# Mamba's decay rows: a product with 64 rows of the array against one with 128, the rest filled with zeros

## The chip, the cores and the metric

The kernel runs on one core of one Trainium2 chip. The metric is the device time of one execution in microseconds (us), as the median of several runs.

## The reference

The kernel computes ten layers in one launch, on 256 tokens of width 1024 in float32: feed-forward layers, one Mamba-2 mixer and three attention mixers, each behind an RMS norm with shift and scale, and each added to the residual with a gate. The change touches the Mamba mixer alone. What matters of it (SSM_CHUNK is 256, so the 256 tokens are one chunk; there are 8 groups of 4 heads):

```python
def step(state, inp):
    x_k, dt_k, b_k, c_k = inp
    acum = jnp.cumsum(dt_k * a, axis=1)
    seg = acum[:, :, None] - acum[:, None, :]
    decay = jnp.exp(jnp.where(causal, seg, -jnp.inf))
    cb = jnp.einsum('btgn,bsgn->btsg', c_k, b_k)
    w = cb[..., None] * decay * dt_k[:, None]
    y_intra = jnp.einsum('btsgr,bsgrp->btgrp', w, x_k)
    ...
```

For each of the 32 heads there is thus a matrix of 256 x 256 decays, exp(acum[t] - acum[s]) for t >= s.

## The kernel before

Float32 products are made out of float32r ones: each operand is split into a high part and a rest, and three products (high x high, high x rest, rest x high) are added in one bank of PSUM. Weights come from DRAM as blocks of 128x2048 through six buffers (`raw`). ScalarE copies a block to its high part (`w_hi`, L495), VectorE subtracts that to get the rest (`w_lo`, L913), both two blocks ahead of TensorE. A third of a block's products are on L1573, L1574 and L1575 each (for the first slice of the inner dimension L1630, L1631 and L1632), with 128 rows, 128 columns of weights and 256 columns that stream.

Each engine has its own program, written out by hand, and works through it in order; engines wait for one another on counters, one per kind of step. `k.wait(name, ...)` waits for such a counter and `k.inc(name, instruction)` raises it.

**The Mamba stage** is the second of ten. It runs a first part and then seven groups of the same form (`body`), each with four blocks of weights. TensorE's program of a group is: the product for x of this group into bank 4; `more_rows`, the decay rows of heads 2 and 3 of the group ahead; the product for B and C into bank 5; `y_out`, the output of the group ahead (L1857, L1858); the product for z into bank 7; `parts`, transposes and C.B (L1832 to L1837); `gemm_out`, the output product of the group before; `first_rows`, the decay rows of heads 0 and 1 of this group. Behind the last group come `more_rows` and `y_out` once more.

**Decay rows** are made by `rows`. The cumulative sums of all 32 heads lie in `acT`, heads on partitions: the high parts on partitions 0 to 31, the rests on 32 to 63. For each group VectorE multiplies them by a column of ones and zeros that keeps the group's four heads (`group_rows`, L1296) and writes `acg`, 64 x 384. The 384 columns are tokens 0 to 255 and once more 128 to 255, for the two halves of the matrix with only what is not above the diagonal. For head h TensorE multiplies `acg` by the selector `sel[:, h * 128:(h + 1) * 128]`, which has a one where a partition's head is h modulo 4: that spreads the head's row (high part plus rest) over all 128 partitions of the bank (L1822). A second product with bf16 operands adds a large negative number above the diagonal: `ident_b` and `below_b`, both in the tile `conb`, 256 columns (L1825). ScalarE then takes the exponential of the bank with a bias for each partition (L650), and VectorE multiplies it by C.B (L1264). `first_rows` and `more_rows` call `rows` twice each, so these products come in pairs, 16 pairs in all.

The selector and the mask are made once, in the first stage, by `mixer_constants`: on ScalarE (L472 to L477, `sel` from the constant `mod4`) and on VectorE (L903, L905). The constant `mod4` is laid out with 128 partitions, of which 64 to 127 hold zeros:

```python
k = np.arange(64)[:, None] % 32
put("mod4", k % 4 == np.arange(4)[None, :])
```

TensorE's wait for the counters `const` and `late` comes at the end of the first stage.

Of the kernel before, what the change touches and what calls it, by code (L numbers as in the profile page):

```python
# [20 lines left out]
F32 = mybir.dt.float32  # L21
F32R = mybir.dt.float32r
# [5 lines left out]
P = 128  # L28
# [222 lines left out]
def build(nc, weights, mods, params, consts, xin, out, stages=None):  # L251
# [3 lines left out]
    with ExitStack() as ctx:  # L255
        def sb(name, shape, dt=F32):
            return ctx.enter_context(nc.sbuf_tensor(name, shape, dt))
# [29 lines left out]
        small = sb("small", [P, 12])  # L287
        cact = sb("cact", [P, NJOB * 8])
        rstd = sb("rstd", [P, T])
        sel = sb("sel", [64, 512], F32R)  # L290

        acg = sb("acg", [64, 384], F32R)[:, :]
        a_hi = sb("a_hi", [P, 2, T], F32R)
        a_lo = sb("a_lo", [P, 2, T], F32R)
        z_hi, z_lo = h_hi[:, 1:3, :], h_lo_rest[:, 0:2, :]
# [31 lines left out]
        def par_(name, at=0, n=None):  # L327
            o, w = PARAMS[name]
            return par[:, o + at:o + at + (w if n is None else n)]

        def con_(name, rows=P):
            o, w = CONSTS[name]
            return con[0:rows, o:o + w]
# [120 lines left out]
        def _(eng):  # L454
# [13 lines left out]
            def mixer_constants():  # L468

                eng.wait_ge(s_con, 16)  # L470
                eng.wait_ge(s_par, 16)
                eng.activation(ident_b, con_("ident"), ACT.Copy)  # L472
                eng.activation(above_b, con_("triL"), ACT.Copy, scale=-NEG)
                m4 = con_("mod4", 64)
                eng.activation(sel[:, :].rearrange("p (h c) -> p h c", h=4), m4.unsqueeze(2).to_broadcast([64, 4, P]),
                               ACT.Copy)
                eng.activation(ws_hi[:, :], par_("wsmall"), ACT.Copy).then_inc(sems["const"], 1)  # L477

# [56 lines left out]
            def ffn(st):  # L535
# [23 lines left out]
                for n in range(1, NFB):  # L559
                    gate(n, 3, -1)  # L560
                    up(n, 3, 0)
                    down(n, 3, 1)
                    if st == 0 and n == GATE_AT:
                        mixer_constants()
                    if st == 0 and n == GATE_AT + 1:
                        gate_weights(1)
# [328 lines left out]
        def _(eng):  # L895
# [4 lines left out]

            def mixer_constants():
                eng.wait_ge(s_con, 16)
                eng.tensor_scalar(below_b, con_("tri"), 1.0, -NEG, ALU.subtract, ALU.mult).then_inc(sems["late"], 1)  # L903
                eng.wait_ge(sems["const"], 1)
                eng.tensor_tensor(ws_lo[:, :], par_("wsmall"), ws_hi[:, :], ALU.subtract).then_inc(sems["late"], 1)  # L905
# [197 lines left out]
            def ffn(st):  # L1103
# [26 lines left out]
                for n in range(1, NFB):  # L1130
                    gate(n, 3, -1)
                    gather(st, n, "gate")
                    up(n, 3, 0)
                    gather(st, n, "up")
                    if st == 0 and n == GATE_AT + 1:
                        mixer_constants()
                    down(n, 3, 1)
                    gather(st, n, "down")
# [416 lines left out]
        def _(eng):  # L1555
# [232 lines left out]
            def mamba(st):  # L1788
# [29 lines left out]
                def rows(i, off, h, free):  # L1818

                    free()  # L1820
                    b = bank[6 + h % 2]
                    eng.matmul(b[:, 0:384], sel[:, h * P:(h + 1) * P], acg, start=True, stop=False,  # L1822
                               skip_group_check=True)
                    diag = b[:, :].rearrange("p (a b c) -> p a b c", a=2, b=2)[:, :, 0, :]
                    k.inc("br", eng.matmul(diag, ident_b, below_b.unsqueeze(1).to_broadcast([P, 2, P]),  # L1825
                                           start=False, stop=True, skip_group_check=True))
# [12 lines left out]
                def first_rows(i):  # L1839
                    if i == 0:  # L1840
                        k.wait("acv", st, b=2)
                    k.wait("acg", st, i, 1, 0)
                    rows(i, 0, 0, lambda: k.wait("y1", st, i, 1, -1))
                    rows(i, 0, 1, lambda: k.wait("sil", st, i, 3, 2))

                def more_rows(i):
                    rows(i, -1, 2, lambda: k.wait("dec", st, i, 4, -4))
                    rows(i, -1, 3, lambda: k.wait("dec", st, i, 4, -3))
# [387 lines left out]
```

## Time and profile before

| | |
|---|---|
| median of 3 runs | 1782.38 us (1781.78 to 1782.6) |
| span of the profiled execution, first to last instruction | 1789.0 us |
| its mean granted clock of TensorE | 0.999 |
| TensorE busy | 1749.9 us (98%) |
| VectorE busy | 1452.8 us (81%) |
| ScalarE busy | 956.5 us (53%) |
| moved from DRAM | 423.74 MB, 239 GB/s over the span |

For the profiled execution no time is given beside its span, which is 6.6 us longer than the median of the runs. Durations below are of that execution. A busy engine is one with an instruction in hand: the records of products overlap, since the next one starts to stream before the one ahead has left the array, so the distance from start to start tells more than a product's own length.

### The profile page before, as it was taken

The page shows a single profiled execution, that of the slowest core. Times are in us where ns is not written, and L with a number is a line of the kernel's source. Part 1 is how long each engine was busy: PE and PEld are TensorE (multiplying, and loading weights), DVE is VectorE, ACT ScalarE, POOL GpSimd, SP SyncE. Part 2 cuts the span into 40 slices and gives each one's busy share as a digit, 9 for nine tenths or more (in the row PEclk, how much of TensorE's full clock was granted, in tenths as well). Part 3 has the DMA queues.
Part 4 walks back from the last instruction along what each step waited for, and adds up shares of the span by engine and source line. Part 5 has one row for each costly group of instructions (what it writes and reads, how often), then busy time and mean ns, then how long its engine had stood idle before and what let it go on. Part 6 is the DMA issues. An engine that isn't in the chain of part 4 may idle for free.

```text
span 1789.0 us, 34260 instructions
## 1 busy us (share of the span) xinstructions
PE 1749.9 (98%) x14686; PEld 1700.5 (95%) x14686; DVE 1452.8 (81%) x1749; ACT 956.5 (53%) x1254; POOL 0.2 (0%) x4
## 2 busy tenths in 40 slices
PE   5999999999999999999999999999999999999999
PEld 4999999998999999999999999999999998989999
DVE  7799898888898889898557989765899887567766
ACT  4443466665533354445766444565655556775553
POOL 0000000000000000000000000000000000000000
PEclk9999999999999999999999999999999999999999
DMA  9998834344597949895444989343288545415551
GB/s 396 414 419 307 322 141 154 134 173 154 219 410 312 373 167 386 326 393 193 170 152 186 388 329 378 134 163 139 110 304 292 206 147 177 151 73 214 187 197 37
DMA packets 68149, 426.23 MB, mean 238 GB/s; under 512 B 7488, under 2 KB 10832, under 8 KB 31824
## 3 DMA queue, kind: packets, MB, share of 16 engines
q1 hardware_dynamic: 63936, 416.22, 60.5%
q10 hardware_dynamic: 4112, 8.62, 1.4%
q8 instruction: 68, 1.11, 0.2%
q14 instruction: 33, 0.27, 0.0%
HBM read 423.74 MB, written 3.17 MB: 239 GB/s over the span
## 4 chain that ended last, share of the span: by engine, by line
PE 90%; DVE 4%; ACT 3%; DMA 2%; issue 0%; DVEq 0%; SPq 0%; ACTq 0%
PE bank L1573 24%; PE bank L1574 24%; PE bank L1575 24%; PE bank L1630 2%; PE bank L1632 2%; PE bank L1631 2%; DMA raw<-weights 1%; PE bank L1686 1%; PE bank L1989 1%; DMA mix<-mods 1%; PE bank L1586 1%; PE bank L1600 1%; PE bank L1589 1%; PE bank L1822 1%; ACT w_hi L495 1%; DVE work L1034 1%
## 5 line engine op out<-in xcount | busy, mean ns | idle before, releaser
L1573 PE MATMUL bank<-h_hi,w_hi 128*128 128x256 f32 x2504 | 696.0, 278 | 0.0
L1574 PE MATMUL bank<-h_lo_rest,w_hi 128*128 128x256 f32 x2504 | 694.9, 278 | 0.0
L1575 PE MATMUL bank<-h_hi,w_lo 128*128 128x256 f32 x2504 | 694.8, 277 | 0.0
L913 DVE TENSOR_TENSOR w_lo<-raw,w_hi 128x2048 fp32r<-128x2048 f32 x267 | 609.5, 2284 | 90.4 <-ACT w_hi L495 89.3
L495 ACT ACTIVATE w_hi<-raw 128x2048 fp32r<-128x2048 f32 x276 | 527.9, 1913 | 160.0 <-PE bank L1575 145.7
L1573 PEld LDWEIGHTS bank<-h_hi,w_hi 128*128 128x128 f32 x2504 | 472.8, 189 | 0.0
L1574 PEld LDWEIGHTS bank<-h_lo_rest,w_hi 128*128 128x128 f32 x2504 | 470.2, 188 | 0.0
L1575 PEld LDWEIGHTS bank<-h_hi,w_lo 128*128 128x128 f32 x2504 | 470.1, 188 | 0.0
L1573 PE MATMUL bank<-a_hi,w_hi 128*128 128x256 f32 x1280 | 358.5, 280 | 1.2 <-DVE a_lo L1291 0.8
L1575 PE MATMUL bank<-a_hi,w_lo 128*128 128x256 f32 x1280 | 355.3, 278 | 0.0
L1574 PE MATMUL bank<-a_lo,w_hi 128*128 128x256 f32 x1280 | 355.3, 278 | 0.0
L1573 PEld LDWEIGHTS bank<-a_hi,w_hi 128*128 128x128 f32 x1280 | 241.9, 189 | 3.4 <-issue 1.4
L1574 PEld LDWEIGHTS bank<-a_lo,w_hi 128*128 128x128 f32 x1280 | 240.4, 188 | 0.1
L1575 PEld LDWEIGHTS bank<-a_hi,w_lo 128*128 128x128 f32 x1280 | 240.4, 188 | 0.0
L968 DVE SCALAR_TENSOR_TENSOR macc<-modws,cact,macc 128x1536 f32<-128x1536 f32 x126 | 225.8, 1811 | 1.8 <-DMA modws<-mods 1.8
L1154 DVE SCALAR_TENSOR_TENSOR mix<-bank,par,mix 128x254 f32<-128x254 f32 (+1 forms) x176 | 76.7, 477 | 41.6 <-ACT mix L581 40.0
L1630 PE MATMUL bank<-h_lo_first,w_hi 128*128 128x256 f32 x344 | 100.1, 291 | 1.6 <-DVE work L1376 1.4
L554 ACT ACTIVATE a_hi<-mix 128x512 fp32r<-128x512 f32 x40 | 25.3, 633 | 140.6 <-PE bank L1575 125.3
L1632 PE MATMUL bank<-h_hi,w_lo 128*128 128x256 f32 x344 | 97.9, 285 | 0.0
L1631 PE MATMUL bank<-h_hi,w_hi 128*128 128x256 f32 x344 | 96.6, 281 | 0.0
L581 ACT ACTIVATE mix<-bank,par 128x256 f32<-128x256 f32 x88 | 44.9, 561 | 92.2 <-PE bank L1575 92.2
L540 ACT ACTIVATE mix<-bank 128x512 f32<-128x512 f32 x44 | 26.4, 599 | 116.8 <-PE bank L1575 116.8
(303 smaller groups left out, 1989.4 us busy)
## 6 DMA issues: line engine op xcount, KB each, us to landing
raw<-weights SPq DMA_DIRECT2D x276, 1024.0 KB, 5.4
modws<-mods SPq DMA_DIRECT2D x144, 768.0 KB, 6.6
mix<-mods SPq DMA_DIRECT2D x5, 1024.0 KB, 8.8
mix<-mods ACTq DMA_DIRECT2D x8, 512.0 KB, 13.3
biases<-scratch ACTq DMA_DIRECT2D x1, 2048.0 KB, 13.1
mix<-biases ACTq DMA_DIRECT2D x4, 512.0 KB, 4.0
modws<-mods SPq DMA_DIRECT2D x1, 1024.0 KB, 11.7
x<-xin SPq DMA_DIRECT2D x1, 1024.0 KB, 10.9
```

The costliest lines, as they stand in the source:

```text
L495: eng.activation(w_hi[g % NW][:, :], raw[g % NRAW][:, :], ACT.Copy).then_inc(sems["whi"], 1)
L540: k.inc("silu", eng.activation(sg, bank[4][:, :].rearrange("p (a t) -> p a t", a=2), ACT.Silu))
L581: ins = eng.activation(dst[:, m, :], b[:, m * T:(m + 1) * T], ACT.Identity, scale=cw(i, t, 2), bias=cw(i, t, 3))
L913: eng.tensor_tensor(w_lo[g % NW][:, :], raw[g % NRAW][:, :], w_hi[g % NW][:, :], ALU.subtract).then_inc(sems["wlo"], 1)
L968: ins = eng.scalar_tensor_tensor(out=m, in0=modw[q % 4], scalar=c, in1=m, op0=ALU.mult, op1=ALU.add)
L1154: ins = eng.scalar_tensor_tensor(out=dst[:, m, lag:T], in0=b[:, m * T:(m + 1) * T - lag], scalar=cw(i, 22 * up + m, tap), in1=dst[:, m, la ...
L1573: eng.matmul(dst, ah, bh, start=start, stop=False, skip_group_check=skip)
L1574: eng.matmul(dst, ah, bl, start=False, stop=False, skip_group_check=skip)
L1575: return eng.matmul(dst, al, bh, start=False, stop=stop, skip_group_check=skip)
L1630: eng.matmul(d, hi[:, kk, part], h_lo(kk), start=True, stop=False)
L1631: eng.matmul(d, hi[:, kk, part], h_hi[:, kk, :], start=False, stop=False)
L1632: eng.matmul(d, lo[:, kk, part], h_hi[:, kk, :], start=False, stop=False)
```

## The change

Both operands of the selector product get 128 partitions. `sel` and `acg` are declared with 128; `acg` stays as the name of the lower 64, into which VectorE writes as before. Partitions 64 to 127 of `sel` are written with the zeros of `mod4` by the same copy on ScalarE, and those of `acg` are cleared once by a new instruction of VectorE. The product takes all 128 partitions of both. The upper half adds zero times zero. No instruction changes its place on any engine, and no wait is added: VectorE has one instruction more, a memset of 64x384 in `mixer_constants`, ahead of the mask constant.

```diff
@@ build @@
-        sel = sb("sel", [64, 512], F32R)
-
-        acg = sb("acg", [64, 384], F32R)[:, :]
+        sel = sb("sel", [P, 512], F32R)
+
+        acg_all = sb("acg", [P, 384], F32R)[:, :]
+        acg = acg_all[0:64, :]
@@ ScalarE, mixer_constants @@
-                m4 = con_("mod4", 64)
-                eng.activation(sel[:, :].rearrange("p (h c) -> p h c", h=4), m4.unsqueeze(2).to_broadcast([64, 4, P]),
+                m4 = con_("mod4")
+                eng.activation(sel[:, :].rearrange("p (h c) -> p h c", h=4), m4.unsqueeze(2).to_broadcast([P, 4, P]),
                                ACT.Copy)
@@ VectorE, mixer_constants @@
                 eng.wait_ge(s_con, 16)
+                eng.memset(acg_all[64:P, :].bitcast(F32), 0.0)
                 eng.tensor_scalar(below_b, con_("tri"), 1.0, -NEG, ALU.subtract, ALU.mult).then_inc(sems["late"], 1)
@@ TensorE, rows @@
-                    eng.matmul(b[:, 0:384], sel[:, h * P:(h + 1) * P], acg, start=True, stop=False,
+                    eng.matmul(b[:, 0:384], sel[:, h * P:(h + 1) * P], acg_all, start=True, stop=False,
                                skip_group_check=True)
```

## Rows read from the trace of the kernel before

**Rows 1.** The page: span, and busy time, share of the span, instructions by engine.

```profile
span 1789.0 us, 34260 instructions
PE 1749.9 (98%) x14686; PEld 1700.5 (95%) x14686; DVE 1452.8 (81%) x1749; ACT 956.5 (53%) x1254; POOL 0.2 (0%) x4
```

**Rows 2.** The page: the chain that ended last, by engine.

```profile
PE 90%; DVE 4%; ACT 3%; DMA 2%; issue 0%; DVEq 0%; SPq 0%; ACTq 0%
```

**Rows 3.** Busy time by stretches: where the memset comes, and one group of Mamba.

```profile
core 0: us, PE busy (x) PEld busy (x) DVE busy (x) ACT busy (x) POOL busy (x), PEclk, DMA share, GB/s
...
64.00:80.00 16.00, 15.64 (x135) 15.45 (x135) 15.22 (x14) 8.58 (x11) 0.00 (x0) 1.00 1.00 413
...
304.00:331.00 27.00, 27.00 (x224) 25.32 (x224) 23.40 (x34) 17.57 (x23) 0.00 (x0) 1.00 0.41 157
```

**Rows 4.** Timeline of TensorE's products around one pair: start us, us, what.

```profile
303.52 0.28 PE L1574 MATMUL bank<-a_lo,w_hi 128*128 128x256 f32 x1
303.63 0.28 PE L1575 MATMUL bank<-a_hi,w_lo 128*128 128x256 f32 x1
303.84 0.44 PE L1822 MATMUL bank<-acg,sel 64*128 64x384 f32 x1
304.21 0.28 PE L1825 MATMUL bank<-conb 128*128 128x256 bf16 x1
304.43 0.44 PE L1822 MATMUL bank<-acg,sel 64*128 64x384 f32 x1
304.80 0.28 PE L1825 MATMUL bank<-conb 128*128 128x256 bf16 x1
...
305.04 0.28 PE L1631 MATMUL bank<-h_hi,w_hi 128*128 128x256 f32 x1
```

**Rows 5.** Timeline of the weight loads (PEld) of the same stretch.

```profile
303.52 0.19 PEld L1575 LDWEIGHTS bank<-a_hi,w_lo 128*128 128x128 f32 x1
303.84 0.18 PEld L1822 LDWEIGHTS bank<-acg,sel 64*128 64x128 f32 x1
304.21 0.10 PEld L1825 LDWEIGHTS bank<-conb 128*128 128x128 bf16 x1 [0.19 <-issue]
...
304.80 0.20 PEld L1630 LDWEIGHTS bank<-h_lo_first,w_hi 128*128 128x128 f32 x1
```

**Rows 6.** Timelines of other stages: bf16 of 384 columns, and plain f32.

```profile
1501.57 0.33 PE L1946 MATMUL bank<-conb 128*128 128x384 bf16 x1
1501.73 0.28 PE L1908 MATMUL bank<-con,mix 128*128 128x1 f32 x2
...
1171.26 0.59 PE L1961 MATMUL bank<-mix,con 128*128 128x256 f32 x2
1171.69 0.27 PE L1962 MATMUL bank<-mix,con 128*128 128x128 f32 x1
```

**Rows 7.** The selector product: ns min/median/max, first and last start.

```profile
L1822 PE MATMUL bank<-acg,sel x32: 407/439/442, 249.2 to 442.2; 64*128 64x384 f32 x32
```

**Rows 8.** Timeline of TensorE at the first pair.

```profile
249.24 0.41 PE L1822 MATMUL bank<-acg,sel 64*128 64x384 f32 x1 [1.15 <-DVE acg L1296]
...
250.40 0.28 PE L1631 MATMUL bank<-h_hi,w_hi 128*128 128x256 f32 x1
```

**Rows 9.** Timeline at the last two pairs: exponentials, and the third selector product.

```profile
440.77 2.84 ACT L650 ACTIVATE work<-bank,mix 128x256 f32<-128x256 f32 x8 [3.44 <-PE bank L1825]
...
441.55 0.44 PE L1822 MATMUL bank<-acg,sel 64*128 64x384 f32 x1 [0.24 <-ACT work L650]
```

**Rows 10.** Timelines of VectorE and TensorE in the group behind the first.

```profile
269.07 0.69 DVE L1291 TENSOR_TENSOR a_lo<-work,a_hi 128x512 fp32r<-128x512 f32 x1
...
270.95 0.36 PE L1573 MATMUL bank<-a_hi,w_hi 128*128 128x256 f32 x1
```

**Rows 11.** VectorE: the multiply of 64x384, and a wait in the first stage.

```profile
L1296 DVE TENSOR_SCALAR acg<-mix,con x8: 400/403/413, 248.7 to 429.9; 64x384 fp32r<-64x384 f32 x8
...
94.92 1.82 DVE L968 SCALAR_TENSOR_TENSOR macc<-modws,cact,macc 128x1536 f32<-128x1536 f32 x1 [0.70 <-DMA modws<-mods]
```

## The prediction

> **What bounds the kernel now.** The shares of the page come first: TensorE is busy for 98% of the span, VectorE for 81% [rows 1]. The chain that ended last runs over TensorE for 90% of its length [rows 2]. So nearly every microsecond that TensorE spends is one of the kernel, whether it multiplies or only stands between two products, as long as the others keep up. The table by stretches then shows the place of the change: in one group of the Mamba stage (27 us, seven such groups follow the first) TensorE is busy throughout at a granted clock of 1.00, while VectorE works 23.4 us of them and ScalarE 17.6 [rows 3]. Busy is not the same as streaming, though. For that one reads the timeline, start by start.
>
> The timeline of one pair of decay rows [rows 4] holds the argument. In the big products 256 columns follow each other every 0.11 us (303.52 to 303.63). Then the steps are: last big product to the first selector product 0.21; selector product to mask product (L1825) 0.37; mask to second selector product 0.22; selector to mask 0.37; mask to the second big product behind it 0.24, in which lie two products of 256 columns, so no pause. Both steps *into* a selector product (64 rows) are 0.10 to 0.11 longer than what 256 columns take, and both steps *out* of it are long as well. The loads say why [rows 5]: the load of a full product starts while the one ahead streams (303.52 for the product at 303.63; the load at 304.80 starts together with the mask product ahead of it), and these loads take 0.19 us at a distance of 0.11. The two loads next to a selector product do not: the selector's load starts 0.21 after the product ahead, and the mask's load stands idle for 0.19 us behind the selector, in which no other engine is named. What distinguishes the three is the number of rows, 64 against 128.
>
> **What the change does, part by part.**
>
> *The product with 128 rows.* Its columns stay 384. The nearest row with 384 columns and full rows is a bf16 product of another stage: 0.16 us from start to start (1501.57 to 1501.73) [rows 6]. Float32r streams as bf16 does, since 256 columns take 0.11 in both. I take 0.16. The other end: plain f32 products with full rows take 0.43 for two of 256 columns (1171.26 to 1171.69) [rows 6], twice as long a column, so 0.32 for 384.
>
> *The pauses.* If they belong to the change between 64 and 128 rows, a pair becomes 0.11 + 0.16 + 0.11 + 0.16 + 0.24 = 0.78 us, where rows 4 have 1.41 (303.63 to 305.04): 0.63 us saved, namely 0.10 + 0.21 + 0.11 + 0.21. The page on tiling of the Trainium skill (TensorEngine Tiling (Array Packing), Key Properties) says that changing the tiling mode drains TensorE; by that rule the trace agrees. The same skill also speaks against the change: TensorE: Matmul & The Clock Gate, in its table on why this matters, has a product of few rows take the same time as one of 128, by which filling up rows would bring nothing and the time would stay 1782.4. That is the first rival below.
>
> *How many.* There are 32 selector products [rows 7], 16 pairs; 13 stand between big products as in rows 4 and read alike to 0.01 us. 13 x 0.63 = 8.2. The first pair waits 1.15 us for VectorE's decay rows and then takes 1.16 (249.24 to 250.40) [rows 8]; after the wait it would take 0.67, 0.5 saved. The last two pairs stand back to back, and behind them ScalarE's exponentials run without a break for 2.84 us [rows 9]; the third selector product and what follows wait for those. There only what lies ahead of the first exponential counts: one step in and one out, 0.3. Sum: 8.2 + 0.5 + 0.3 = 9.0 us.
>
> *What is late next.* The groups become 1.26 us shorter, 26 instead of 27.25, against 23.4 us of VectorE's work [rows 3]: it has idle time left. It is tightest in the group behind the first, where VectorE runs without a pause: its rest of the gated output (L1291) ends at 269.76, and TensorE begins the product that reads it at 270.95 [rows 10], 1.2 us later. By then TensorE is ahead by 0.5 + 0.6 = 1.1. That eats the slack almost wholly; with the signal between the engines I put 0.1 us of waiting. In later groups TensorE gains at most 1.26 per group while VectorE's own inputs come earlier too, since they hang on TensorE; I cost these at nothing, and if that cover is gone it is rival two.
>
> *The added clearing on VectorE.* One memset of 64x384 ahead of the mask constant, before the Mamba stage. No row shows one; above it is bounded by the multiply of the same shape, 0.40 us [rows 11], below by nothing much, say 0.1. I take 0.3, nearer to the same shape. It comes at about 79 us, where VectorE is busy 15.2 of 16 us and the DMA queues are full [rows 3]. Behind it stand the splitting of weights and the accumulation that frees modulation buffers; a later free buffer is a later transfer, and lost DMA time there is not regained at once. But VectorE waits 0.70 us for such a transfer at 94.92 [rows 11], so most is absorbed. Between 0 and 0.4, I take 0.1. The selector's copy on ScalarE has as many elements in each row as before and more rows: nothing, and if it did cost, ScalarE is the engine with the most idle time.
>
> So 9.0 - 0.1 - 0.1 = 8.8 us. The profiled execution spans 1789.0 us, 6.6 above the median of the runs, 1782.4; the pauses are differences within it, and I subtract them from the median: **1773.6**. About 0.2%, 3.6 us, is what a measurement of this kernel can tell from no change, so faster means below 1778.8.
>
> **The rivals.**
>
> *No gain: the pause isn't of rows.* The long steps could belong to the order float32r, bf16, float32r with different shapes, or to the bank the pair writes twice. For it: every selector product stands beside a mask product. Against: the mask product is followed by a full float32r product without pause (304.80 to 305.04), and the step into the selector from a float32r product (0.21) is the same as from a bf16 one (0.22). Time: 1782.4 plus at most 0.4 for the clearing, 1782.6. Chance 0.08.
>
> *The gain is made on TensorE and partly eaten.* If VectorE, now at 23.4 of 26 us, makes TensorE wait about 0.5 us in each of seven groups (the gap at rows 10 fully used, again and again), 3.5 go: 8.8 - 3.5 = 5.3, 1777.1. For: VectorE takes its work in order, with weights to split in the middle. Against: no wait of TensorE between 276 and 440. Chance 0.08.
>
> *Half the pauses stay.* Suppose the selector's load cannot be pulled ahead even with full rows. Then the steps in remain: 13 x 0.21, 0.1 in the first pair and 0.1 in the last, about 2.9; the gain is 5.9 and the time 1776.5. The reverse, that only the steps in go, gives 1779.5. TensorE: Matmul & The Clock Gate of the Trainium skill (Part 3, What overlaps and what doesn't) has weight loads overlap running products only where their row groups differ; by that rule the full load would stay exposed, but rows 5 show full loads overlapping full products. Chance 0.08 for both, half on each side of 1778.8.
>
> *Slower: the full product streams at the rate of plain f32.* The place is L1822, the price 32 x (0.32 - 0.16) = 5.1 us of TensorE time. It decides the sign if the pauses don't go: 1782.4 + 5.1 = 1787.5; if they go, it leaves 1778.7. For it only the longer record of the selector product [rows 7], against it the float32r products with full rows at 0.11 for 256 columns [rows 4]. Chance 0.04 for the first.
>
> **How the numbers follow.** The forecast has what is left, 0.72. Its own bounds: 16 x 0.63 = 10.1 with nothing eaten gives 1772.3; with the spread of the runs (0.4) and a step a little shorter than I took, 1771.5. The range reaches up over the two partial cases to 1779.0 and leaves out no gain (0.08), slower (0.04) and a bit of the partial ones. Faster: 0.72 + 0.08 + 0.04 = 0.84. Within 0.2%: 0.08 + 0.04 = 0.12. Slower: 0.04.
>
> **What would show it.** In the profile of the changed kernel the mask's load should have no idle time before it, the steps around a pair should read 0.11, 0.16, 0.11, 0.16, and the distance between the same places of two groups 26.0 us instead of 27.25. The first rival shows unchanged steps of 0.37; the second shows short steps and new waits of TensorE for VectorE in the Mamba stage; the third short steps on one side alone; the fourth a step of 0.32 behind the selector. I am wrong if a pair takes over 1.0 us, or if TensorE's waits in the stage grow by more than a microsecond.

## The result, and the profile after

The median of 21 executions is 1773.94 us, against 1783.16 us for 21 of the kernel before. The ratio of changed to before is 0.9953, with a 95% interval from 0.9939 to 0.9967: some 8.4 us, or 0.47%, faster, and clear of the 0.2% that a measurement can tell. The forecast was 1773.6 us. Both medians are raised by executions in which a stage ran at a slower pace (below), 10 of 21 before and 7 of 21 with the change. The others have medians of 1782.01 and 1773.55 us, 8.5 apart.

The page of the changed kernel, its span, the busy times and the chain that ended last (lines from 287 on have moved by one or two: L1822 is L1824, L1825 is L1827):

```profile
span 1782.0 us, 34261 instructions
PE 1742.4 (98%) x14686; PEld 1699.3 (95%) x14686; DVE 1452.5 (82%) x1750; ACT 956.5 (54%) x1254; POOL 0.2 (0%) x4
...
PE 93%; DVE 3%; ACT 3%; DMA 1%; issue 0%; DVEq 0%; SPq 0%; ACTq 0%
```

But for the one memset the instructions are what they were, and so is the bound [rows 1, 2]; TensorE is busy for 7.5 us less. The timeline of TensorE around one pair of decay rows, to be laid beside [rows 4]:

```profile
303.79 0.28 PE L1577 MATMUL bank<-h_hi,w_lo 128*128 128x256 f32 x1
303.90 0.34 PE L1824 MATMUL bank<-acg,sel 128*128 128x384 f32 x1
304.09 0.28 PE L1827 MATMUL bank<-conb 128*128 128x256 bf16 x1
304.12 0.42 PE L1824 MATMUL bank<-acg,sel 128*128 128x384 f32 x1
304.39 0.28 PE L1827 MATMUL bank<-conb 128*128 128x256 bf16 x1
...
304.63 0.28 PE L1633 MATMUL bank<-h_hi,w_hi 128*128 128x256 f32 x1
```

And its weight loads, to be laid beside [rows 5]:

```profile
303.80 0.19 PEld L1824 LDWEIGHTS bank<-acg,sel 128*128 128x128 f32 x1
304.08 0.10 PEld L1827 LDWEIGHTS bank<-conb 128*128 128x128 bf16 x1
304.09 0.20 PEld L1824 LDWEIGHTS bank<-acg,sel 128*128 128x128 f32 x1
```

The selector's load now starts together with the big product ahead of it, and the mask's load has lost its idle time, in all 32 cases. (Single steps inside the pair read oddly: the second selector is recorded 0.03 us behind the mask, and 0.27 lie between it and the next mask. From mask to mask it is 0.30.) The pair takes 304.63 - 303.79 = 0.84 us instead of 1.41. One group behind another comes after 26.09 us (297.70 to 323.79 for the same place) instead of 27.25.

**Which part of two profiles can be compared.** The spans of the two profiled executions differ by 7.0 us, but they can't be subtracted. Every feed-forward stage runs, from its start to its end, at one of two paces, and which one it is changes from execution to execution, in both kernels alike. The number of big products that start in 100 us shows it: first before, then changed, a stretch in the first and one in the sixth stage (us, TensorE busy and in brackets the products, clock, DMA share, GB/s).

```profile
80.00:180.00 100.00, 100.00 (x852) 1.00 0.94 368
970.00:1070.00 100.00, 100.00 (x880) 1.00 0.89 350
```

```profile
80.00:180.00 100.00, 100.00 (x879) 1.00 0.96 377
970.00:1070.00 100.00, 100.00 (x852) 1.00 0.90 349
```

From start to start that is 117.8 against 114.0 ns a product on average (a window also counts the products under way at its start), 3.7 us up to the first selector product where the first stage was hit (249.24 against 245.50), some 5 us in a later stage; the slower pace had hit the first stage of the one profile and the sixth of the other (and the third of both). So the change is read within Mamba alone: from the first selector product to the first product of the last output it is 443.03 - 249.24 = 193.79 us before and 430.93 - 245.50 = 185.43 us after. That is 8.36 us less, about the measured gain of 8.4.

Not all of it is the change. Mamba has the two paces too, there for each stretch of some 45 big products between two interruptions. The kernels differ in this only in the first three stretches: from the first pair to the second the kernel before takes 255.81 - 250.40 = 5.41 us and the changed one 251.62 - 246.36 = 5.26, and in the next two the differences cancel. So 0.15 us is pace. Another 0.09 is gone again a few products later: read to the second pair of heads of the last output, at 443.76 and 431.75, the difference is 8.27. The change is worth **8.1 us** within the stage.

### The profile page after: what moved, and what is told of

The parts are those of the page before. It is cut to its first block, busy times and chain, and to the rows that moved or that the text cites. A ratio compares the mean times of both kernels' runs of the same rounds, so it can differ in the third digit from the quotient of the medians.

```text
span 1782.0 us, 34261 instructions
## 1 busy us (share of the span) xinstructions
PE 1742.4 (98%) x14686; PEld 1699.3 (95%) x14686; DVE 1452.5 (82%) x1750; ACT 956.5 (54%) x1254; POOL 0.2 (0%) x4
## 4 chain that ended last, share of the span: by engine, by line
PE 93%; DVE 3%; ACT 3%; DMA 1%; issue 0%; DVEq 0%; SPq 0%; ACTq 0%
PE bank L1575 25%; PE bank L1576 24%; PE bank L1577 24%; PE bank L1632 2%; PE bank L1634 2%; PE bank L1633 2%; PE bank L1588 1%; PE bank L1688 1%; PE bank L1602 1%; PE bank L1991 1%; DMA mix<-mods 1%; PE bank L1591 1%; ACT w_hi L496 1%; PE bank L1859 1%; ACT work L719 0%; PE bank L1972 0%
## 5 line engine op out<-in xcount | busy, mean ns | idle before, releaser
L541 ACT ACTIVATE mix<-bank 128x512 f32<-128x512 f32 x44 | 26.4, 600 | 117.8 <-PE bank L1577 117.7
```

Source lines behind the costliest of these rows:

```text
L541: k.inc("silu", eng.activation(sg, bank[4][:, :].rearrange("p (a t) -> p a t", a=2), ACT.Silu))
```

## The experiments

A pair, below, is the time from the start of the last big product ahead of it to the start of the second one behind it: 1.41 us before, 0.84 us with the change. The pairs of one kernel agree to about 0.01 us. Single times of executions are given but carry no verdict, since an execution may hold stages at the slower pace (up to two in the profiled ones).

### All four products of a pair on 64 rows (e1_mask64)

From the kernel before. The mask product takes 64 rows as well, with operands of its own; both diagonal blocks are then blanked instead of masked.

```diff
-                    k.inc("br", eng.matmul(diag, ident_b, below_b.unsqueeze(1).to_broadcast([P, 2, P]),
+                    k.inc("br", eng.matmul(diag, fold_b[:, :], neg_b[:, :].unsqueeze(1).to_broadcast([64, 2, P]),
```

> Kernel before, with the mask product also on 64 rows, so that all four products of a pair have 64 rows. It leaves out the right mask: both diagonal blocks are blanked instead. Read from the start of the last big product ahead of a pair to the second behind it (before: 1.41 us, changed kernel: 0.84). Theory A, the pause belongs to the change between 64 and 128 rows: only one step in and one out are left, 0.21 + 0.17 + 0.11 + 0.17 and about 0.45 at the way out, 1.1 us in all, and the mask's load stands idle no more behind the selector inside the pair. Theory B, the pause belongs to the selector product or to the alternation of float32r and bf16: the steps of 0.37 stay, 1.4 us.

Measured (1779.22 us, once). The timeline of TensorE around a pair; L1825 is the selector, L1828 the mask:

```profile
278.15 0.28 PE L1578 MATMUL bank<-h_hi,w_lo 128*128 128x256 f32 x1
278.35 0.44 PE L1825 MATMUL bank<-acg,sel 64*128 64x384 f32 x1
278.64 0.28 PE L1828 MATMUL bank<-neg_b,fold_b 64*128 64x256 bf16 x1
278.94 0.28 PE L1828 MATMUL bank<-neg_b,fold_b 64*128 64x256 bf16 x1
279.15 0.39 PE L1633 MATMUL bank<-h_lo_first,w_hi 128*128 128x256 f32 x1
279.37 0.28 PE L1634 MATMUL bank<-h_hi,w_hi 128*128 128x256 f32 x1
```

The pair takes 1.22 us. Inside it float32r and bf16 still take turns, but the first selector is followed by its mask after 0.29 instead of 0.37 and the second mask comes 0.30 behind the first, exactly as in the changed kernel (304.09 to 304.39). The pauses are now at the two ends: 0.20 on the way in, and on the way out the full product's load waits until 279.15. So neither the selector product as such nor the change of types has the price; the change of size has it. Theory A's 1.1 us was short by 0.12, all of it at the first selector: from there to its mask it is 0.29 us, not the forecast 0.17, while the way out takes 0.43 (forecast 0.45). On the way in the selector starts 0.09 late, and its own load of 0.18 us then costs another 0.11. So the pause holds the load of the next product, and its price goes with that load. A change ahead of a float32r load (0.18 to 0.19 us) costs 0.20 here on the way in and 0.19 on the way out. A change ahead of the mask's bf16 load (0.10 us) costs 0.08, the 0.37 of the kernel before less these 0.29. Twice 0.20 and twice 0.08 make 0.56, the excess of 0.57 of the pair before.

### Half as many changes of size (e2_adjacent)

From the kernel before, same results: the two selectors of a pair stand next to each other.

```diff
-                    eng.matmul(b[:, 0:384], sel[:, h * P:(h + 1) * P], acg, start=True, stop=False,
-                               skip_group_check=True)
+                    last = h % 2
+                    for step in (("spread", "mask") if last else ("mask", "spread")):
...
```

> Kernel before, same products and results, in the order mask, selector, selector, mask instead of selector, mask, selector, mask. Theory A: two changes of size a pair instead of four: 0.11 + 0.22 + 0.16 + 0.37 + 0.24 = 1.10 us instead of 1.41, a gain of 0.3 a pair, about 4.5 us in the stage. Theory B, a fixed price for each 64-row product: 1.41 as before. If the price sits in the alternation of types, also 1.10, which e1 then tells apart (there the types still alternate).

Measured (1779.86 us, once). The timeline of TensorE; L1826 stands for both selectors, with one mask ahead of them and one behind:

```profile
306.65 0.28 PE L1575 MATMUL bank<-h_hi,w_lo 128*128 128x256 f32 x1
...
306.98 0.61 PE L1826 MATMUL bank<-acg,sel 64*128 64x384 f32 x2
...
307.77 0.28 PE L1631 MATMUL bank<-h_hi,w_hi 128*128 128x256 f32 x1
```

1.12 us, forecast 1.10. The same four products on the same rows, with two changes of size instead of four: half the excess over 0.84 is gone (0.28 is left of 0.57). A change costs 0.14 us here, on average; by e1 it is 0.20 into the selectors and 0.08 out of them.

### 96 rows (e3_rows96)

From the changed kernel; `sel[0:96, ...]` and `acg_all[0:96, :]` in the product.

> Changed kernel, but the selector product takes 96 rows instead of 128 (results the same). If up to 64 rows count as one size and more as full, the pair takes 0.84 us as in the changed kernel. If every row count short of 128 has its own size, the pauses are back: 1.41 us.

Measured (1777.54 us, once). The timeline of TensorE:

```profile
277.27 0.28 PE L1577 MATMUL bank<-h_hi,w_lo 128*128 128x256 f32 x1
277.39 0.34 PE L1824 MATMUL bank<-acg,sel 96*128 96x384 f32 x1
...
278.12 0.28 PE L1633 MATMUL bank<-h_hi,w_hi 128*128 128x256 f32 x1
```

0.85 us: 96 rows count as full ones. What mattered was not to fill up to the last row but to leave the size of 64 behind. Between 65 and 95 nothing was tried.

### Only heads 0 and 1 (e4_first_only)

From the changed kernel; `r = slice(0, P if h < 2 else 64)` picks the rows of both operands.

> Changed kernel with full rows for heads 0 and 1 alone (the pairs of first_rows); the pairs of more_rows go back to 64 rows. One part alone, both kinds in one trace: first_rows 0.84 us, more_rows 1.41, a group 26.67 us (27.25 before, 26.09 changed), the first selector product to the last output 4.1 us less than before instead of 8.4. If the gain came from anything set up once (the clearing, the wider copy), both kinds would read alike.

Measured (1782.11 us, once). In one trace, first_rows and then the next more_rows:

```profile
272.01 0.28 PE L1577 MATMUL bank<-a_hi,w_lo 128*128 128x256 f32 x1
272.12 0.34 PE L1825 MATMUL bank<-acg,sel 128*128 128x384 f32 x1
...
272.85 0.28 PE L1633 MATMUL bank<-h_hi,w_hi 128*128 128x256 f32 x1
```

```profile
278.10 0.28 PE L1577 MATMUL bank<-h_hi,w_lo 128*128 128x256 f32 x1
278.30 0.44 PE L1825 MATMUL bank<-acg,sel 64*128 64x384 f32 x1
...
279.50 0.28 PE L1633 MATMUL bank<-h_hi,w_hi 128*128 128x256 f32 x1
```

0.84 and 1.40 us, side by side. Five groups take 411.43 - 278.10 = 133.33 us, 26.67 each, as expected; first selector to last output is 434.89 - 245.33 = 189.56 us, 4.2 less than before. Nothing that is set up once has a part in the gain. (The time of this one execution shows no gain: its eighth stage ran at the slower pace, which costs what the four microseconds gave.)

### The preparation alone (e5_clear_only)

From the changed kernel; the product goes back to `sel[0:64, ...]` and `acg`, the clearing and the wider copy stay.

> Changed kernel with the wider selector copy and the clearing of the upper half kept, but the selector product back on 64 rows (results the same): the cost of the preparation alone. Theory A: pairs of 1.41 us as before, groups of 27.25, the memset takes 0.38 us of VectorE and nothing of the end: equal to the kernel before within its spread. A rival, that the memset's delay of weight splitting or of the transfers behind it costs up to 0.4 us or more, would show as new waits of TensorE in the first stage.

Measured: ratio to before 1.0007, interval 0.9994 to 1.002. Pairs of 1.41 us (306.31 to 307.72), and the mask's load again idle for 6.0 us in 32 cases. The memset takes 0.38 us of VectorE; TensorE waits for nothing in the first stage that it did not wait for in other kernels without it. From the first selector product to the last output it takes 193.80 us, 193.79 before. In the trace the preparation costs nothing. The times are a weaker witness: the interval reaches up to 0.2%, 3.6 us, since 8 of the 12 executions lie near 1787 us, as 9 of the 23 of the kernel before do; the other four lie at 1781.1 to 1783.1. Whether that share is chance was not looked into.

### Masks behind both selectors (e6_masks_last)

From the changed kernel: selector, selector, mask, mask, through a function `pair` in place of the two calls of `rows`.

> Changed kernel with the order selector, selector, mask, mask in a pair instead of selector, mask, selector, mask (same results). A pair takes 0.84 us where its streaming gives 0.78. If the remaining 0.06 comes from the bf16 weights behind a float32r product (twice a pair, loads of 0.10 that start only when the selector's stream ends), one such step is left and a pair takes about 0.81. If it comes from the longer stream of the selector alone, 0.84 stays.

Measured (1775.71 us, once). The timeline of TensorE:

```profile
251.47 0.28 PE L1577 MATMUL bank<-h_hi,w_lo 128*128 128x256 f32 x1
251.58 0.52 PE L1821 MATMUL bank<-acg,sel 128*128 128x384 f32 x2
251.94 0.39 PE L1826 MATMUL bank<-conb 128*128 128x256 bf16 x2
...
252.29 0.28 PE L1633 MATMUL bank<-h_hi,w_hi 128*128 128x256 f32 x1
```

0.82 to 0.83 us, between the two expectations. Two selectors take 251.94 - 251.58 = 0.36, so 0.18 each, not the 0.16 of a bf16 product with as many columns [rows 6]: that explains two thirds of the 0.06. The last 0.02 stays open. And the order is no gain but a loss: the stage takes 187.17 us from the first selector to the last output, 1.7 more than with the change, and a group 26.25 instead of 26.09. The big products behind a pair have gone over to the slower pace, in nearly every group:

```profile
301.60 0.28 PE L1575 MATMUL bank<-h_hi,w_hi 128*128 128x256 f32 x1
...
303.72 0.28 PE L1575 MATMUL bank<-h_hi,w_hi 128*128 128x256 f32 x1
```

Eighteen products take 2.12 us, 117.8 ns each; the same eighteen in the changed kernel take 303.56 - 301.52 = 2.04. So what stands ahead of a stretch bears on its pace.

### The same remedy for columns (e7_full_columns)

From the changed kernel. Mamba's output multiplies with 64 weight columns a head; here zeros stand beside them, and two heads add up in one block of the bank.

```diff
-                        eng.matmul(bank[6][rows_, c0:c0 + T], xdt[:, 0, ch], S[:, h, 0:T], start=True, stop=False)
+                        eng.matmul(bank[6][:, c0:c0 + T], xdt[0][:, ch], S[:, h, 0:T], start=not odd, stop=False,
+                                   skip_group_check=True)
...
```

> Changed kernel plus the same remedy for the columns: the 64 weight columns of each head in the output of Mamba (L1859, L1860) get 64 columns of zeros beside them, so that those products use all 128 columns of the array and add up in one bank; VectorE writes its operand in two instructions instead of one. Theory A, the pause belongs to any change of the part of the array in use: from the last big product ahead to the second behind it 1.93 us now, 1.55 then; 8 times 0.38, some 3 us less than the changed kernel, 1771 us. Rival: columns have no such pause and the long steps there are of plain f32 products: 1.93 stays and the time is 1774 us.

Measured: 1780.97 us (ratio to before 0.999, interval 0.9977 to 1.0003): 7 us *slower* than the changed kernel. Both theories fall. First the output in the changed kernel, then in this one (L1865 and L1867 are its products):

```profile
309.88 0.28 PE L1577 MATMUL bank<-h_hi,w_lo 128*128 128x256 f32 x1
310.08 0.66 PE L1859 MATMUL bank<-work,mix 128*64 128x256 f32 x4
310.57 0.40 PE L1860 MATMUL bank<-work,mix 128*64 128x128 f32 x4
...
311.81 0.28 PE L1633 MATMUL bank<-h_hi,w_hi 128*128 128x256 f32 x1
```

```profile
311.69 0.28 PE L1583 MATMUL bank<-h_hi,w_lo 128*128 128x256 f32 x1
311.80 0.59 PE L1865 MATMUL bank<-work,mix 128*128 128x256 f32 x2
312.23 0.38 PE L1867 MATMUL bank<-work,mix 128*128 128x128 f32 x2
...
314.54 0.29 PE L1639 MATMUL bank<-h_hi,w_hi 128*128 128x256 f32 x1
```

The pause is gone indeed (0.11 instead of 0.20 on the way in), but the whole takes 2.85 us instead of 1.93. In the changed kernel four records of 256 columns take 0.49 us (0.43 for the second two heads, 310.79 to 311.22), here two take 0.43. And four records in a row at L1859, where the program has one product of each shape a head (two records each): the heads 0 and 1 run *at the same time*. 8 x 0.92 = 7.4 us is about what the time lost.

### Is it the neighbours that share the array? (e8_heads_0213, e9_both_halves)

e8: the changed kernel with heads in the order 0, 2, 1, 3, so that the first two and the last two want the same half of the columns.

```diff
-                    for h in range(4):
+                    for h in (0, 2, 1, 3):
```

> Changed kernel with the heads of Mamba's output in the order 0, 2, 1, 3 instead of 0, 1, 2, 3 (same results, columns left at 64). e7 made that output longer, 2.85 us from the last big product ahead to the second behind, instead of 1.93. Theory C: products of heads 0 and 1 take different halves of the array's columns and run at the same time; filling up took that away. Then neighbours in the same half (0 and 2, 1 and 3) run one after the other: 2.3 to 2.8 us. Rival: a product of 64 columns is just faster than one of 128: the order does not matter, 1.93.

e9: the order of e2, with the second selector and its rows in partitions 64 to 127.

```diff
+                    eng.tensor_scalar(acg, acT, col, None, ALU.mult)
+                    k.inc("acg", eng.tensor_scalar(acg_up, acT, col, None, ALU.mult))
...
+                            half = slice(64 * last, 64 * last + 64)
+                            mm = eng.matmul(b[:, 0:384], sel[half, h * P:(h + 1) * P], acg_all[half, :], start=last == 1,
```

> Kernel before in the order mask, selector, selector, mask (as e2, whose pairs take 1.12 us), but the second selector and its decay rows lie in partitions 64 to 127, so that the two products of 64 rows take different halves of the array's rows (same results; VectorE writes the rows twice, ScalarE the selector twice). If two such products run at the same time, the second costs almost nothing and a pair takes 1.12 - 0.16 = about 0.95 us; that is still more than the 0.84 of full rows. If products of different row halves come one after the other, 1.12, and if their change of place costs a pause too, 1.3.

Measured (1787.53 and 1776.99 us, once each; e8 has its third and its last stage at the slower pace). The output in e8:

```profile
310.91 0.28 PE L1577 MATMUL bank<-h_hi,w_lo 128*128 128x256 f32 x1
311.12 0.65 PE L1859 MATMUL bank<-work,mix 128*64 128x256 f32 x2
...
311.82 0.65 PE L1859 MATMUL bank<-work,mix 128*64 128x256 f32 x4
...
312.53 0.59 PE L1859 MATMUL bank<-work,mix 128*64 128x256 f32 x2
...
313.49 0.28 PE L1633 MATMUL bank<-h_hi,w_hi 128*128 128x256 f32 x1
```

2.58 us with the same products. Head 0 runs alone (two records), then heads 2 and 1 together (four records, 0.43 us as two of them take alone), then head 3 alone. Only neighbours in different halves run together. The pair in e9:

```profile
304.90 0.28 PE L1578 MATMUL bank<-h_hi,w_lo 128*128 128x256 f32 x1
...
305.23 0.45 PE L1830 MATMUL bank<-acg,sel 64*128 64x384 f32 x2
...
305.86 0.28 PE L1634 MATMUL bank<-h_hi,w_hi 128*128 128x256 f32 x1
```

0.96 us, expected 0.95, where e2 took 1.12: two selectors of 64 rows in different halves take the time of one. So the rows behave like the columns. It still loses to full rows by 0.12 us, since both pauses stay. No version tried is better than the changed kernel.

## Why the prediction was right

- **What bounds the kernel, and the pause.** Right. The pause belongs to the change between 64 and 128 rows: shown by e1 (four products of one size, no pause between them), e2 (half the changes, half the excess) and e4 (both kinds in one trace). The rival "no gain" falls with the time, and its causes with e1. The Trainium skill's sentence on draining (TensorEngine Tiling (Array Packing), Key Properties) agrees with these runs. The rule of the Trainium skill that a product of few rows takes as long as a full one (TensorE: Matmul & The Clock Gate, Why this matters for your kernels) is true of the product (0.30 us from mask to mask in e1 as in the changed kernel), and silent on its neighbours.
- **The size of a pair.** Forecast 0.63 us saved, measured 0.57. The term that was mis-sized is "I take 0.16" for the full selector: it streams in 0.18 (e6), 0.04 in a pair; 0.02 more is open. 13 x 0.57 = 7.4 instead of 8.2. The forecast also put the pauses on the wrong sides, 0.10 in and 0.21 out, where e1 shows 0.20 and 0.08. And the steps it named as a sign, 0.11, 0.16, 0.11 and 0.16, read 0.11, 0.19, 0.03 and 0.27; only their sum is near.
- **The ends of the stage.** The first pair: 0.5 forecast, 0.3 measured (245.50 to 246.36 is 0.86, instead of 1.16):

```profile
245.50 0.41 PE L1824 MATMUL bank<-acg,sel 128*128 128x384 f32 x1 [1.15 <-DVE acg L1298]
...
246.36 0.28 PE L1633 MATMUL bank<-h_hi,w_hi 128*128 128x256 f32 x1
```

  The first selector's step is 0.26 us even with full rows: behind a wait its own load stands exposed. The way out is 0.06 longer than elsewhere, for which no cause is shown. The last pairs: 0.3 forecast. ScalarE's eight exponentials (L651) start 428.75 - 428.14 = 0.61 us behind the last big product, instead of 440.77 - 439.87 = 0.90: 0.3, and all that follows hangs on them, as the forecast had it (compare [rows 9]).
- **What is late next.** The tight place was the right one. In the group behind the first VectorE now goes from L1293 to L1330 with no idle time, where it had 0.81 us:

```profile
265.33 0.69 DVE L1293 TENSOR_TENSOR a_lo<-work,a_hi 128x512 fp32r<-128x512 f32 x1
265.94 0.68 DVE L1330 TENSOR_TENSOR mix<-bank,mix 128x512 f32<-128x512 f32 x1
```

  But TensorE does not wait there: the 0.1 us I put were not taken. L1293 ends at 266.02 and the product behind it starts at 266.18, so 0.16 us are left of the 1.2 [rows 10]. The rival of a gain that is partly eaten falls: the only wait of TensorE that grew in this stage is the one for the exponentials at the end of the stage (0.52 instead of 0.24), which belongs to the 0.3 above.
- **The clearing.** 0.38 us on VectorE where I took 0.3, and nothing of it at the end (e5) where I took 0.1.
- **The sum.** Forecast 8.8, worth within the stage 8.1. Thirteen pairs gave 7.5 (0.57 us each and 0.01 behind each: a group is 1.16 us shorter, two pairs), the first pair 0.3 and the end of the stage 0.3. Against the forecast the pairs gave 0.7 less and the first pair 0.2 less, and the 0.2 subtracted for a wait and for the clearing were not lost. That the median of the times came within 0.3 us of the forecast is luck: the ratio's interval alone is some 5 us wide.
- **The rivals with half the pauses and with the rate of plain f32** fall with the timeline after: steps are short on both sides, and the selector streams in 0.18, not 0.32. The rule of the Trainium skill that loads overlap running products only where row groups differ (TensorE: Matmul & The Clock Gate, What overlaps and what doesn't) does not hold here: full loads of 0.19 us start every 0.11 us while full products run [rows 5]. What delays a load here is a change of size.

## What to carry to other kernels

Read the distance from start to start, not busy time: a product with 64 rows between full ones costs a pause on both sides, in which the engine counts as busy, and zeros up to more than 64 rows (96 was enough) remove both for nothing. Before filling up, look whether the narrow products have a neighbour in the other half: two of 64 rows or columns in different halves run at the same time, and filling those up costs more (0.92 us net for each output here, e7) than the pauses do. Where both halves are used, the order of the neighbours is worth as much as the pause (0.65 us an output, e8). And look at the pace of the big products behind what you changed: in e6 it took back more than the order had gained.

## What was not expected of the hardware

- Two products of 64 columns, or of 64 rows, in different halves of the array take the time of one (e8: four records in 0.43 us; e9: 0.96 us a pair instead of 1.12). It was in the trace of before, as runs of four records, and I passed it over.
- A feed-forward stage runs at 114.0 or at 117.8 ns for each product of 256 columns, the same from its start to its end, at a granted clock of 1.00 in both. It fell on other stages from profile to profile: the first and third before, the third and sixth with the change, the eighth in e3 and e4, the third in e5, the third and tenth in e8, none in e1, e2, e6, e7 and e9. It spreads the times of both kernels in steps of some 5 us (before: about 1782, 1787 and 1792; changed: about 1773, 1779 and 1783).
- In Mamba each stretch of some 45 big products between two interruptions has one of the same two paces. In the changed kernel the stretch behind each output is a slow one; in e6 that one is fast, and those behind most pairs are slow. The pace thus goes with how a stretch begins. What it is in that beginning that sets it was not tested.
